# Taking the two softmax halves of block one's attention in turns

## The chip, the cores and the metric

The kernel runs on one core of a Trainium2 chip. The metric is the device time of one execution in microseconds. A core has five engines with instruction queues of their own, each worked off in the order in which the program wrote it: TensorE (PE) for matmuls, VectorE (DVE), ScalarE (ACT), GpSimd (POOL) and SyncE (SP), which issues the transfers of the weights. They wait for one another through semaphores.

## The reference

Two transformer blocks run one after the other on 256 tokens of width 1024. The change is in the first block's mixer. Its input projection feeds three things: an attention with three dilation groups and four heads, an RWKV-7 time mixing with eight heads, and the gates that merge the two.

```python
z = u @ w_in[i]                                  # attention, RWKV and gate columns
s = einsum('bqhd,bqjhd->bqhj', qb, kg) * scale   # for each of 3 groups
s = where(valid, s, -inf)
m = max(s);  e = exp(s - m);  den = sum(e);  o = e @ v / den;  lse = m + log(den)
alpha = softmax(stack(lses))                     # the three groups merged
o = alpha[0] * o0 + alpha[1] * o1 + alpha[2] * o2
...
merged = sigmoid(gate_attn) * (o_attn @ w_attn_up) + sigmoid(gate_rwkv) * (o_rwkv @ w_rwkv_up)
```

Weighting the groups with alpha is the same as one softmax over the scores of all three groups side by side, with masks. The kernel computes it that way.

## The kernel before

Attention is worked off in four rounds: query block `i` (0 or 1, 128 queries each) times head pair `hh` (0 or 1). A round holds two heads, the halves `par` 0 and 1. The scores of one half are 384 columns wide in the rounds of query block 0 and 768 in those of query block 1. The text calls the rounds (0,0), (0,1), (1,0) and (1,1).

Every engine has an `attention()` generator of the same steps, in which each `yield` ends a step:

- **Scores step.** TensorE writes the scores of both halves to PSUM (L1258). VectorE adds the mask and takes the row minimum of the negated, scaled scores for both halves (L2811; two pieces for each half in query block 1, the event is called `r`). ScalarE takes the exponential of both halves with a row sum (L1726, event `x`).
- **Next step.** VectorE waits for `x` of each half, takes the reciprocal of the row sum (L2818) and scales the half (L2417, event `e`). TensorE and ScalarE do nothing for attention here.
- **Two transpose steps**, one for each half. TensorE waits for `e` of that half and transposes it (L707), and ScalarE copies it out of PSUM (L1729, event `t`).
- **An empty step and the value step** (L1301), which ScalarE copies out.

`turns.paired(gates(), attention())` sets one step of the gate projection (six matmuls, L701 to L703) ahead of each attention step, and `turns.mix` alternates these with the steps of `rwkv()`, in the part looked at here strictly one for one. Since the generators of all engines are driven by the same sequence of turns, this sequence is also the order on each engine's queue, and an engine never passes an instruction that waits. In the RWKV chain, one step solves a level with matmuls L1131 and L1134, VectorE masks the result in two instructions (L2744, event `T`), the next step multiplies with L1147 and its neighbours, and ScalarE copies it out (event `X`). VectorE also makes the low parts of the gate weights, 1024 columns at a time (L2471, "split" below).

PSUM banks go round in rings. Attention takes them from `pa` = banks 2, 3, 4, and RWKV from `rw_bank` = banks 4, 5, 6, 7. So bank 4 is in both rings. TensorE keeps in `free[b]` the event that releases bank b and waits for it before it writes the bank again. In query block 1 the scores of a round lie in three banks, released so (`bs` are the three banks, the pairs are half and piece):

```python
for b, event in zip(bs, ((0, 0), (1, 0), (1, 1))):
    free[b] = [at_dve.at("r", i, hh, *event)]
```

In round (1,0) `bs` is 3, 4, 2, and in round (1,1) it is 2, 3, 4. The waits that this puts on TensorE ahead of the RWKV product L1147, two steps behind the scores, are `r` of half 1, piece 0 in round (1,0), and `r` of half 1, piece 1 in round (1,1), each beside `T`.

Of the kernel before, what the change touches and what calls it, by code (L numbers as in the profile page):

```python
# [242 lines left out]
def bc(ap, n):  # L243
    return ap.unsqueeze(2).broadcast_to([ap.shape[0], ap.shape[1], n])
# [30 lines left out]
def program(nc, A, consts, vecs, pt, out):  # L275
    with ExitStack() as ctx:
# [54 lines left out]
        def const(off, n):  # L331
            return low[:, OC + off:OC + off + n]
# [1383 lines left out]
        def scalar_program(e, turns):  # L1716
# [3 lines left out]
            def bank(b):  # L1720
                return PSUM[:, b, :]

            def act(o, a, f, bias=0.0, scale=1.0, accum=None):
                if accum is None:
                    return e.activation(o, a, f, bias=bias, scale=scale)  # L1725
                return e.activation(o, a, f, bias=bias, scale=scale, accum_out=accum)  # L1726

            def copy(o, a):
                return e.activation(o, a, ACT.Copy)  # L1729
# [294 lines left out]
            def attention():  # L2024
                yield
                for i in range(2):
                    for hh in range(2):
                        W, nb = 128 * (i + 1), 3 * (i + 1)
                        for _ in range(i + 2):
                            next(pa)  # L2030
                        for par in range(2):
                            q.wait_ge(*at_dve.at("r", i, hh, par, i))
                            s = at_sm[par][:, 0:3 * W]
                            act(s, s, ACT.Exp, scale=-1.0, bias=sm_at[par][0][:, i:i + 1], accum=sm_at[par][1]) \
                                .then_inc(at_act.up("x", i, hh, par), 1)
                        yield
                        yield
                        for par in range(2):
                            for b0 in range(0, nb, 4):
                                k = min(4, nb - b0)  # L2040
                                p = bank(next(pa))
                                q.wait_ge(*at_pe.at("t", i, hh, par, b0))
                                copy(at_eT[par][:, 128 * b0:128 * (b0 + k)], p[:, 0:128 * k]).then_inc(at_act.up("t", i, hh, par, b0), 1)
                            yield
                        yield
                        p = bank(next(pa))
                        q.wait_ge(*at_pe.at("o", i, hh))
                        copy(o_attn[:, hh, 128 * i:128 * i + 128], p[:, 0:128]).then_inc(at_act.up("o", i, hh), 1)
                        yield
# [16 lines left out]
            def fills():  # L2066
                yield from qkv()
                yield from turns.paired(gates(), attention())
                for _ in range(4):
                    turns.go("up", ups)  # L2070
                    yield
# [335 lines left out]
        def vector_program(e, turns):  # L2407
# [3 lines left out]
            def bank(b):  # L2411
                return PSUM[:, b, :]
# [3 lines left out]
            def ts(o, a, s1, s2, op0, op1):  # L2416
                return e.tensor_scalar(o, a, s1, s2, op0, op1) if op1 is not None else e.tensor_scalar(o, a, s1, None, op0)  # L2417
# [370 lines left out]
            def attention():  # L2788
                ma = const(C_MA, 768)
                yield  # L2790
                for i in range(2):
                    for hh in range(2):
                        W, nb = 128 * (i + 1), 3 * (i + 1)
                        bs = [bank(next(pa)) for _ in range(i + 2)]
                        for par in range(2):
                            sm = at_sm[par]
                            nm, den, rden = sm_at[par]
                            q.wait_ge(*at_pe.at("s", i, hh, par))
                            if i == 0:
                                pieces = [(bs[par][:, 0:384].rearrange("p (g t) -> p g t", g=3),  # L2800
                                           ma.rearrange("p (g w t) -> p g w t", g=3, w=2)[:, :, 1, :],
                                           sm[:, 0:384].rearrange("p (g t) -> p g t", g=3))]
                            elif par == 0:
                                pieces = [(bs[0], ma[:, 0:512], sm[:, 0:512]), (bs[1][:, 0:256], ma[:, 512:768], sm[:, 512:768])]
                            else:
                                pieces = [(bs[1][:, 256:512], ma[:, 0:256], sm[:, 0:256]), (bs[2], ma[:, 256:768], sm[:, 256:768])]
                            for n, (ps, mask, dst) in enumerate(pieces):
                                if n:
                                    q.wait_ge(*at_dve.at("r", i, hh, par, n - 1))
                                    q.wait_ge(*at_pe.at("s", i, hh, 1))  # L2810
                                e.tensor_tensor_reduce(dst, ps, mask, -0.125, 3e38 if n == 0 else nm[:, n - 1:n], ALU.add, ALU.min,  # L2811
                                                       nm[:, n:n + 1]).then_inc(at_dve.up("r", i, hh, par, n), 1)
                        yield
                        for par in range(2):
                            sm = at_sm[par]
                            nm, den, rden = sm_at[par]
                            q.wait_ge(*at_act.at("x", i, hh, par))
                            e.reciprocal(rden, den).then_inc(at_dve.up("rd", i, hh, par), 1)  # L2818
                            q.wait_ge(*at_dve.at("rd", i, hh, par))
                            ts(sm[:, 0:3 * W], sm[:, 0:3 * W], rden, None, ALU.mult, None).then_inc(at_dve.up("e", i, hh, par), 1)  # L2820
                        yield
                        for par in range(2):
                            for b0 in range(0, nb, 4):
                                next(pa)
                            yield
                        yield
                        next(pa)
                        yield
# [23 lines left out]
            def fills():  # L2852
                yield from qkv()
                yield from turns.paired(gates(), attention())
                for _ in range(4):
                    turns.go("up", ups)
                    yield
# [193 lines left out]
            def maxima(done_d, done_p, name, E, banks, W, mask, nm):  # L3051
                for h in range(4):
                    q.wait_ge(*done_p.at(name[0], h % 2))
                    o = 256 * (h // 2)
                    e.tensor_tensor_reduce(E[:, h, :], banks[h % 2][:, o:o + W], mask, -0.125, 3e38, ALU.add, ALU.min, nm[:, h:h + 1]) \
                        .then_inc(done_d.up(name[0], h), 1)

            def scaled(done_a, done_d, name, E, W, den, rden, gate):
                q.wait_ge(*done_a.at(name[1], 3))
                e.reciprocal(rden, den).then_inc(done_d.up(name[2], "r"), 1)  # L3060
                q.wait_ge(*done_d.at(name[2], "r"))
                if gate is not None:
                    tt(rden, rden, gate, ALU.mult).then_inc(done_d.up(name[2], "g"), 1)
                    q.wait_ge(*done_d.at(name[2], "g"))
                tt(E, E, bc(rden, W), ALU.mult).then_inc(done_d.up(name[2]), 1)
# [570 lines left out]
```

## Time and profile before

| | |
|---|---|
| median of 3 runs | 964.19 us (964.15 to 964.5) |
| time of the profiled execution | 963.96 us |
| its span, first to last instruction | 962.1 us |
| granted TensorE clock, mean | 0.998 |
| attention rounds of the first block | about 154 to 234 us into the span |

The span is 1.86 us shorter than the time of the same execution. The profiled execution is 0.23 us below the median. All rows below are of the profiled execution; a row's time is counted from the start of the span.

### The profile page before, as it was taken

The page shows a single profiled execution, that of the slowest core. Times are in us where ns is not written, and L with a number is a line of the kernel's source. Part 1 is how long each engine was busy: PE and PEld are TensorE (multiplying, and loading weights), DVE is VectorE, ACT ScalarE, POOL GpSimd, SP SyncE. Part 2 cuts the span into 40 slices and gives each one's busy share as a digit, 9 for nine tenths or more (in the row PEclk, how much of TensorE's full clock was granted, in tenths as well). Part 3 has the DMA queues.
Part 4 walks back from the last instruction along what each step waited for, and adds up shares of the span by engine and source line. Part 5 has one row for each costly group of instructions (what it writes and reads, how often), then busy time and mean ns, then how long its engine had stood idle before and what let it go on. Part 6 is the DMA issues. An engine that isn't in the chain of part 4 may idle for free.

```text
span 962.1 us, 15665 instructions
## 1 busy us (share of the span) xinstructions
PE 930.7 (97%) x6744; PEld 765.4 (80%) x6744; DVE 574.3 (60%) x906; ACT 427.2 (44%) x682; POOL 43.9 (5%) x60
## 2 busy tenths in 40 slices
PE   7999999999999999999999999999999999999997
PEld 5999887777658988888879988765677698888885
DVE  1568765754373566655764567865572456666673
ACT  2674344355132344444642446463341435554571
POOL 1010000100000000000000350000000000000000
PEclk9999999999999999999999999999999999999999
DMA  9445332222545855555347674433456456665531
GB/s 336 124 129 174 95 126 89 63 72 89 204 170 191 244 177 185 204 181 198 122 161 167 153 227 132 132 112 107 169 182 171 131 156 177 186 195 189 178 128 44
DMA packets 131205, 150.79 MB, mean 157 GB/s; under 512 B 11808, under 2 KB 102176, under 8 KB 131008
## 3 DMA queue, kind: packets, MB, share of 16 engines
q1 hardware_dynamic: 129920, 145.57, 48.7%
q10 hardware_dynamic: 1216, 4.23, 1.2%
q8 instruction: 53, 0.87, 0.4%
q14 instruction: 16, 0.13, 0.0%
HBM read 148.73 MB, written 1.05 MB: 156 GB/s over the span
## 4 chain that ended last, share of the span: by engine, by line
PE 83%; DVE 8%; DMA 3%; ACT 3%; issue 2%; SPq 0%; POOL 0%; POOLq 0%; ACTq 0%
PE psum L812 11%; PE psum L701 9%; PE psum L703 8%; PE psum L702 8%; PE psum L764 6%; PE psum L813 6%; PE psum L784 4%; PE psum L1315 3%; PE psum L785 3%; PE psum L793 3%; PE psum L707 2%; PE psum L870 2%; DMA low<-in_w_in_dram 2%; PE psum L860 2%; PE psum L861 2%
## 5 line engine op out<-in xcount | busy, mean ns | idle before, releaser
L1729 ACT ACTIVATE parts<-low 128x1024 fp32r<-128x1024 f32 (+1 forms) x232 | 235.5, 1047 | 107.4 <-PE psum L703 61.5
L2471 DVE TENSOR_TENSOR parts<-low,parts 128x1024 fp32r<-128x1024 f32 (+1 forms) x146 | 177.3, 1240 | 32.2 <-ACT parts L1729 31.7
L701 PE MATMUL psum<-parts 128*128 128x512 f32 (+2 forms) x424 | 171.1, 404 | 1.0 <-DVE parts L2471 1.0
L703 PE MATMUL psum<-parts 128*128 128x512 f32 (+2 forms) x424 | 163.7, 386 | 0.0
L702 PE MATMUL psum<-parts 128*128 128x512 f32 (+2 forms) x424 | 163.5, 386 | 0.0
L812 PE MATMUL psum<-parts 128*128 128x512 f32 x434 | 155.7, 398 | 0.0
L813 PE MATMUL psum<-parts 128*128 128x256 f32 x496 | 129.2, 281 | 0.0
L1729 ACT ACTIVATE high<-psum 128x512 f32<-128x512 f32 (+4 forms) x102 | 55.8, 565 | 165.0 <-PE psum L815 73.1
L813 PEld LDWEIGHTS psum<-parts 128*128 128x128 f32 x496 | 93.7, 189 | 5.7
L701 PEld LDWEIGHTS psum<-parts 128*128 128x128 f32 x424 | 79.6, 188 | 21.3 <-issue 3.2
L812 PEld LDWEIGHTS psum<-parts 128*128 128x128 f32 x434 | 81.7, 188 | 16.9
L703 PEld LDWEIGHTS psum<-parts 128*128 128x128 f32 x424 | 79.7, 188 | 16.3
L702 PEld LDWEIGHTS psum<-parts 128*128 128x128 f32 x424 | 79.8, 188 | 15.1 <-issue 1.2
L2531 DVE TENSOR_TENSOR parts<-low,parts 128x1024 fp32r<-128x1024 f32 x54 | 66.0, 1221 | 35.3 <-ACT parts L1729 35.3
L764 PE MATMUL psum<-low 128*128 128x128 f32 (+2 forms) x640 | 73.4, 276 | 2.5 <-DVE low L2448 2.4
L764 PEld LDWEIGHTS psum<-low 128*128 128x128 f32 (+2 forms) x640 | 71.9, 188 | 4.2 <-DVE low L2448 3.3
L784 PE MATMUL psum<-parts 128*128 128x256 f32 x264 | 70.0, 300 | 2.1 <-ACT parts L1729 2.1
L785 PE MATMUL psum<-parts 128*128 128x256 f32 x264 | 65.3, 283 | 0.0
L784 PEld LDWEIGHTS psum<-parts 128*128 128x128 f32 x264 | 50.3, 191 | 6.3 <-issue 5.0
L785 PEld LDWEIGHTS psum<-parts 128*128 128x128 f32 x264 | 50.5, 191 | 1.0 <-issue 1.0
L2894 DVE TENSOR_TENSOR mid<-psum,high 128x512 f32<-128x512 f32 x31 | 21.4, 691 | 44.8 <-ACT high L1729 44.8
L860 PE MATMUL psum<-parts 128*128 128x512 f32 x96 | 39.1, 407 | 2.0 <-ACT parts L1725 1.0
(313 smaller groups left out, 1293.9 us busy)
## 6 DMA issues: line engine op xcount, KB each, us to landing
low<-in_w_in_dram SPq DMA_DIRECT2D x40, 1024.0 KB, 5.2
low<-in_w_ffn_in_dram SPq DMA_DIRECT2D x44, 512.0 KB, 5.2
low<-in_w_ff_in_dram SPq DMA_DIRECT2D x16, 1024.0 KB, 5.7
low<-in_w_ff_out_dram SPq DMA_DIRECT2D x16, 1024.0 KB, 4.9
low<-in_w_ffn_out_dram SPq DMA_DIRECT2D x11, 1024.0 KB, 4.9
low<-in_w_out_dram SPq DMA_DIRECT2D x8, 1024.0 KB, 6.3
low<-in_w_ple_gate_dram SPq DMA_DIRECT2D x4, 1024.0 KB, 4.9
low<-in_w_up_dram SPq DMA_DIRECT2D x3, 1024.0 KB, 4.9
```

Source lines behind the costliest of these rows:

```text
L701: mm(o, l[0], r[0], start, False)
L702: mm(o, l[0], r[1], False, False)
L703: return mm(o, l[1], r[0], False, stop)
L764: t = mm(PSUM[0:m, banks[n], 256 * j + 128 * i:256 * j + 128 * i + 128], w3[:, k, off:off + m], uT[:, k, 128 * i:128 * i + 128], k == 0, k ...
L784: mm(o, hi[:, k, c], st.uh[:, k, :], k == 0, False)
L785: mm(o, lo_[:, k, c], st.uh[:, k, :], False, False)
L812: mm(p, hi[:, k, c], st.u2(k), k == 0, False)
L813: mm(p[:, 0:256], lo_[:, k, c], st.uh[:, k, :], False, False)
L860: mm(PSUM[:, banks[n % 2], :], l, hi[:, c], k == 0, False)
L1729: return e.activation(o, a, ACT.Copy)
L2471: tt(rslot3(n, nk, width)[:, r, 0:w], slot3(n, nk, width)[:, r, 0:w], st.hi3(j)[:, r, 0:w].bitcast(F32), ALU.subtract) \
L2531: tt(rview(OR + 2048 * n + 1024 * (k % 2), 1024), slot(n)[:, 1024 * (k % 2):1024 * (k % 2) + 1024], rview(base, 1024).bitcast(F32), ALU.su ...
```

## The change

On VectorE the masked minimum of the second half leaves the scores step and goes to the step behind it, where the scaling of the first half follows; the scaling of the second half goes one step further, to the first transpose step, behind the RWKV step in between. On ScalarE the exponential of the second half goes two steps further, again to the first transpose step, ahead of the copy. TensorE's instructions and their order stay as they are. No instruction is added or taken away.

```diff
--- before.py
+++ after.py
@@ -2028,13 +2028,17 @@
                         W, nb = 128 * (i + 1), 3 * (i + 1)
                         for _ in range(i + 2):
                             next(pa)
-                        for par in range(2):
+
+                        def weights(par):
                             q.wait_ge(*at_dve.at("r", i, hh, par, i))
                             s = at_sm[par][:, 0:3 * W]
                             act(s, s, ACT.Exp, scale=-1.0, bias=sm_at[par][0][:, i:i + 1], accum=sm_at[par][1]) \
                                 .then_inc(at_act.up("x", i, hh, par), 1)
-                        yield
-                        yield
+
+                        weights(0)
+                        yield
+                        yield
+                        weights(1)
                         for par in range(2):
                             for b0 in range(0, nb, 4):
                                 k = min(4, nb - b0)
@@ -2792,7 +2796,8 @@
                     for hh in range(2):
                         W, nb = 128 * (i + 1), 3 * (i + 1)
                         bs = [bank(next(pa)) for _ in range(i + 2)]
-                        for par in range(2):
+
+                        def maxima(par):
                             sm = at_sm[par]
                             nm, den, rden = sm_at[par]
                             q.wait_ge(*at_pe.at("s", i, hh, par))
@@ -2810,16 +2815,23 @@
                                     q.wait_ge(*at_pe.at("s", i, hh, 1))
                                 e.tensor_tensor_reduce(dst, ps, mask, -0.125, 3e38 if n == 0 else nm[:, n - 1:n], ALU.add, ALU.min,
                                                        nm[:, n:n + 1]).then_inc(at_dve.up("r", i, hh, par, n), 1)
-                        yield
-                        for par in range(2):
+
+                        def scaled(par):
                             sm = at_sm[par]
                             nm, den, rden = sm_at[par]
                             q.wait_ge(*at_act.at("x", i, hh, par))
                             e.reciprocal(rden, den).then_inc(at_dve.up("rd", i, hh, par), 1)
                             q.wait_ge(*at_dve.at("rd", i, hh, par))
                             ts(sm[:, 0:3 * W], sm[:, 0:3 * W], rden, None, ALU.mult, None).then_inc(at_dve.up("e", i, hh, par), 1)
+
+                        maxima(0)
+                        yield
+                        maxima(1)
+                        scaled(0)
                         yield
                         for par in range(2):
+                            if par == 1:
+                                scaled(1)
                             for b0 in range(0, nb, 4):
                                 next(pa)
                             yield
```

Line numbers behind the edits rise by 4 on VectorE (L2417 becomes L2421, L2471 L2475, L2744 L2748), by 5 for L2811 and L2818 (now L2816 and L2823).

VectorE in round (0,1), from the RWKV normalisation on; `ISA` is the masked minimum and the read-out of its result, RECIPROCAL and TENSOR_SCALAR on `mid` are the scaling of one half, `parts` are the low parts of gate weights. Before:

```order
L2693 TENSOR_TENSOR high<-high,low 128x512
L2818 RECIPROCAL low<-low 128x1
L2417 TENSOR_SCALAR mid<-mid,low 128x384
L2818 RECIPROCAL low<-low 128x1
L2417 TENSOR_SCALAR mid<-mid,low 128x384
L2727 TENSOR_TENSOR high<-psum,low 128x4x128 x2
L2471 TENSOR_TENSOR parts<-low,parts 128x1024
L2734 TENSOR_TENSOR high<-psum,low 128x512 x2
L2697 TENSOR_REDUCE low<-high 128x8
L2417 TENSOR_SCALAR low<-low 128x8
L2471 TENSOR_TENSOR parts<-low,parts 128x1024
```

The same place with the change:

```order
L2816 ISA mid,low<-psum,low 128x384
L2816 ISA low 128x1
L2823 RECIPROCAL low<-low 128x1
L2421 TENSOR_SCALAR mid<-mid,low 128x384
L2731 TENSOR_TENSOR high<-psum,low 128x4x128 x2
L2475 TENSOR_TENSOR parts<-low,parts 128x1024
L2738 TENSOR_TENSOR high<-psum,low 128x512 x2
L2701 TENSOR_REDUCE low<-high 128x8
L2421 TENSOR_SCALAR low<-low 128x8
L2475 TENSOR_TENSOR parts<-low,parts 128x1024
L2823 RECIPROCAL low<-low 128x1
L2421 TENSOR_SCALAR mid<-mid,low 128x384
```

The first half's scaling now stands behind the second half's minimum (the two ISA rows), and the second half's scaling has moved from the fourth and fifth row of before to behind two splits, both parts of the RWKV masking of L2731, one of L2738 and a reduction.

VectorE in round (1,0), from the first half's second minimum on. Before:

```order
L2811 ISA mid,low<-psum,low 128x256
L2811 ISA low 128x1
L2811 ISA mid,low<-psum,low 128x256
L2811 ISA low 128x1
L2811 ISA mid,low<-psum,low 128x512
L2811 ISA low 128x1
L2744 TENSOR_TENSOR high<-psum,low 64x512 x2
L2709 TENSOR_TENSOR high<-high 128x4x128
L2711 TENSOR_TENSOR high<-high 128x4x128
L2471 TENSOR_TENSOR parts<-low,parts 128x1024
L2818 RECIPROCAL low<-low 128x1
L2417 TENSOR_SCALAR mid<-mid,low 128x768
```

With the change:

```order
L2816 ISA mid,low<-psum,low 128x256
L2816 ISA low 128x1
L2748 TENSOR_TENSOR high<-psum,low 64x512 x2
L2713 TENSOR_TENSOR high<-high 128x4x128
L2715 TENSOR_TENSOR high<-high 128x4x128
L2475 TENSOR_TENSOR parts<-low,parts 128x1024
L2816 ISA mid,low<-psum,low 128x256
L2816 ISA low 128x1
L2816 ISA mid,low<-psum,low 128x512
L2816 ISA low 128x1
L2823 RECIPROCAL low<-low 128x1
L2421 TENSOR_SCALAR mid<-mid,low 128x768
```

The second half's two minima have moved behind the RWKV masking, two RWKV products and a split.

VectorE in round (1,1), before, from the RWKV masking behind the minima on:

```order
L2744 TENSOR_TENSOR high<-psum,low 64x512 x2
L2818 RECIPROCAL low<-low 128x1
L2417 TENSOR_SCALAR mid<-mid,low 128x768
L2818 RECIPROCAL low<-low 128x1
L2417 TENSOR_SCALAR mid<-mid,low 128x768
L2471 TENSOR_TENSOR parts<-low,parts 128x1024
L2744 TENSOR_TENSOR high<-psum,low 64x512 x2
L2471 TENSOR_TENSOR parts<-low,parts 128x1024
```

With the change, from the first scaling on:

```order
L2823 RECIPROCAL low<-low 128x1
L2421 TENSOR_SCALAR mid<-mid,low 128x768
L2475 TENSOR_TENSOR parts<-low,parts 128x1024
L2748 TENSOR_TENSOR high<-psum,low 64x512 x2
L2475 TENSOR_TENSOR parts<-low,parts 128x1024
L2823 RECIPROCAL low<-low 128x1
L2421 TENSOR_SCALAR mid<-mid,low 128x768
```

The second scaling has moved behind a split, the next level's masking and another split.

## Rows read from the trace of the kernel before

**Rows 1.** Page: busy time and share; granted TensorE clock in 40 slices.

```profile
PE 930.7 (97%) x6744; PEld 765.4 (80%) x6744; DVE 574.3 (60%) x906; ACT 427.2 (44%) x682; POOL 43.9 (5%) x60
...
PEclk9999999999999999999999999999999999999999
```

**Rows 2.** Windows: busy time (and count) of each engine in the rounds.

```profile
150.00:235.00 85.00, 79.33 (x1209) 61.87 (x1208) 50.37 (x94) 39.88 (x74) 2.55 (x1) 1.00 0.24 76
```

**Rows 3.** Timeline of PE: start, duration, line, forms, idle before and its releaser.

```profile
158.65 1.14 PE L1166 MATMUL psum<-high 64*64 64x64 f32 x16 [0.43 <-ACT high L1729]
...
182.72 0.55 PE L707 MATMUL psum<-low,mid 128*128 128x128 f32 x3 [0.58 <-DVE mid L2417]
...
185.76 0.49 PE L707 MATMUL psum<-low,mid 128*128 128x128 f32 x3
...
201.45 0.24 PE L1147 MATMUL psum<-high 64*64 64x64 f32 x1 [1.09 <-DVE high L2744]
...
204.67 0.88 PE L707 MATMUL psum<-low,mid 128*128 128x128 f32 x6 [0.46 <-DVE mid L2417]
...
205.47 0.27 PE L1131 MATMUL psum<-high 64*64 64x64 f32 x1
...
208.04 0.82 PE L707 MATMUL psum<-low,mid 128*128 128x128 f32 x6
...
224.15 0.24 PE L1147 MATMUL psum<-high 64*64 64x64 f32 x1 [1.10 <-DVE high L2744]
...
230.05 0.82 PE L707 MATMUL psum<-low,mid 128*128 128x128 f32 x6
```

**Rows 4.** Timeline of ACT in round (0,0).

```profile
156.67 0.62 ACT L1726 ACTIVATE mid<-mid,low 128x384 f32<-128x384 f32 x1 [4.38 <-DVE low L2811]
...
157.29 0.60 ACT L1726 ACTIVATE mid<-mid,low 128x384 f32<-128x384 f32 x1
...
158.00 1.69 ACT L1729 ACTIVATE high<-psum 64x512 f32<-64x512 f32 x3
```

**Rows 5.** Timeline of DVE in round (0,1).

```profile
177.30 0.55 DVE L2811 CUSTOM_DVE_ANT_1 mid<-psum,low 128x384 f32<-128x384 f32 x1
...
182.05 0.15 DVE L2818 RECIPROCAL low<-low 128x1 f32<-128x1 f32 x1
182.24 0.42 DVE L2417 TENSOR_SCALAR mid<-mid,low 128x384 f32<-128x384 f32 x1
...
187.54 1.22 DVE L2471 TENSOR_TENSOR parts<-low,parts 128x1024 fp32r<-128x1024 f32 x1
```

**Rows 6.** Timeline of DVE in round (1,0).

```profile
198.76 0.42 DVE L2811 CUSTOM_DVE_ANT_0 mid<-psum,low 128x256 f32<-128x256 f32 x1
...
199.22 0.75 DVE L2811 CUSTOM_DVE_ANT_0 mid<-psum,low 128x512 f32<-128x512 f32 x1
...
199.90 1.40 DVE L2744 TENSOR_TENSOR high<-psum,low 64x512 f32<-64x512 f32 x2
...
202.67 1.22 DVE L2471 TENSOR_TENSOR parts<-low,parts 128x1024 fp32r<-128x1024 f32 x1
...
203.99 0.62 DVE L2417 TENSOR_SCALAR mid<-mid,low 128x768 f32<-128x768 f32 x1
...
206.65 1.41 DVE L2744 TENSOR_TENSOR high<-psum,low 64x512 f32<-64x512 f32 x2 [1.31 <-PE psum L1134]
208.09 1.22 DVE L2471 TENSOR_TENSOR parts<-low,parts 128x1024 fp32r<-128x1024 f32 x1
```

**Rows 7.** Timeline of DVE in round (1,1).

```profile
228.66 1.41 DVE L2744 TENSOR_TENSOR high<-psum,low 64x512 f32<-64x512 f32 x2 [1.95 <-PE psum L1134]
230.10 1.23 DVE L2471 TENSOR_TENSOR parts<-low,parts 128x1024 fp32r<-128x1024 f32 x1
```

**Rows 8.** Longest waits of PE: line, waited for, us in total, times, longest.

```profile
PE psum L942 <- DMA low<-in_w_ple_dram: 5.3, 1, 5.3
...
PE psum L784 <- ACT parts L1729: 2.1, 2, 1.3
```

## The prediction

> **What bounds the kernel now.** The page comes first: TensorE is busy for 97% of the span, VectorE for 60% and ScalarE for 44% [rows 1]. So another engine counts only where TensorE waits for it, and a wait that TensorE is given in a place where it had none goes into the time whole, unless a later wait of TensorE shrinks by it. The windows narrow this to the stage of the change: in the 85 us around the four rounds TensorE is busy for 79.33 us, so at most about 5.7 us could be won in the stage at all [rows 2]. The timeline of TensorE then shows where it stands idle near the attention steps [rows 3]: 0.43 us at L1166, 0.58 us and 0.46 us at the first half's transposes of rounds (0,1) and (1,0), 1.09 us and 1.10 us at L1147 in rounds (1,0) and (1,1). It also shows what matters more: the second half's transposes L707 at 185.76, 208.04 and 230.05 us begin with no wait. The timelines of VectorE and ScalarE at the same places [rows 4 to 7] say how far ahead of these the event `e` comes, and what the change puts ahead of it.
>
> **The change part by part.** No instruction is added, and TensorE's order stays. Everything turns on four moments for each round: when `r` of the second half frees bank 4 where TensorE waits for that, and when `e` of each half comes, against the start of the transposes that wait for it. I take the rounds in order and count how much later TensorE's next work begins.
>
> *Round (0,0).* ScalarE runs two exponentials from 156.67 and 157.29 and only then, from 158.00, the copies for which L1166 waits [rows 4]. With the second exponential gone from there the copies begin about 0.6 us earlier, and TensorE's idle time of 0.43 us at L1166 [rows 3] goes. The second exponential then runs behind the copies; its transpose is some 6 us away. Term: minus 0.45 us.
>
> *Round (0,1), first half.* TensorE waits at 182.72 for `e`, which comes out of the scaling that starts at 182.24 and takes 0.42 [rows 3, 5]. VectorE is busy without a break ahead of it, and the second half's minimum, 0.55 us [rows 5], now stands right ahead of the reciprocal at 182.05. The place that it leaves at 177.30 is no gain: the RWKV masking behind it needs the matmuls of the same step, which were only just over when it began. Term: plus 0.55 us.
>
> *Round (0,1), second half.* Before, the second scaling followed right on the first. Now it stands behind the second split of the step, which starts at 187.54 and takes 1.22 [rows 5]. What is ahead of that split keeps its length: one scaling went out (0.15 and 0.42 us) and one minimum came in (0.55). So the reciprocal begins at about 188.7, the scaling 0.19 later (182.05 to 182.24), and with 0.42 `e` comes at 189.3, seen by TensorE at about 189.35. TensorE would be at its transposes at 185.76 + 0.55 = 186.3 [rows 3]. It waits for 3.05 us that it did not wait before. Term: plus 3.05 us.
>
> *Round (1,0), bank 4.* L1147 starts at 201.45 after the masking from 199.90 for 1.40 us [rows 3, 6]. The second half's two minima, from 198.76 to 199.90 with their read-outs, no longer stand ahead of that masking, so it moves up by about 1.1 us and ends at about 200.2. But L1147 also waits for the bank that the first piece of the second half's minimum frees, and this piece now stands behind the split. The split moves up by the same 1.1 us, from 202.67 to 201.6, and ends at about 202.75; the piece takes 0.42 (the row at 198.76), so L1147 starts at about 203.25, 1.8 us later than before. The 0.46 us that TensorE waited at 204.67 for the first half's `e` are gone then, since `e` comes at 202.75 + 0.46 (198.76 to 199.22) + 0.75 + 0.19 + 0.62, about 204.8, and the transposes are reached at about 206.0. Term: 1.8 minus 0.46, plus 1.35 us.
>
> *Round (1,0), second half.* Its scaling now stands behind the masking that L1131 releases. L1131 at 205.47 lets it start at 206.65, and what is behind it starts at 208.09 [rows 3, 6]. From 208.09 on, 0.19 + 0.62 bring `e` at 208.9, against transposes that were at 208.04. Both move with TensorE, so the difference stays: plus 0.9 us.
>
> *Round (1,1), bank 4 and first half.* L1147 here waits for the second piece of the second half. VectorE has the same four pieces and the same masking ahead of it in another order, with no split in between, so it ends as before and the 1.10 us at 224.15 stay, perhaps 0.1 more. The first half's `e` still comes a good 1.5 us ahead of its transposes.
>
> *Round (1,1), second half.* Its scaling now stands behind the split that starts at 230.10 and takes 1.23 [rows 7]. `e` comes at 230.10 + 1.23 - 0.1 (an instruction starts a little ahead of the end of the last) + 0.19 + 0.62, about 232.05, and with the 0.1 and the way to TensorE at 232.2, against 230.05 [rows 3]. Term: plus 2.15 us.
>
> On ScalarE the move costs nothing more: the second half's exponential stands where ScalarE would wait for the transposes, and in round (1,1), where it makes the first half's copy some 1.1 us late, the bank that this copy frees is asked for only by the transposes that are themselves 2.1 us late. Were that cover gone, about 1 us would be in the open. The splits of VectorE keep or improve their places. SyncE's transfers are released by TensorE's matmuls and move with them.
>
> **Sum.** -0.45 + 0.55 + 3.05 + 1.35 + 0.9 + 2.15 = 7.55 us. The profiled execution took 963.96 us (span 962.1 and 1.86 around it), which gives 971.5. The median of the runs is 0.23 higher than that execution, less than the terms are good for; I predict 971.5 us.
>
> **Rivals.**
>
> *Less is lost, because something gives it back (12%).* A term fails or the wait is absorbed: the piece or split ahead may have slack that the rows don't show, or a transfer that ran out just in time at a later wait. For it: two terms, 3.05 and 2.15, hang on the order behind one split each. Against it: the stage's own waits total only 5.7 us, and apart from those counted they are for copies behind the same transposes, so they move along. Without the 3.05 us the time is 968.5; without the 2.15 and the 1.35 it is 968.0.
>
> *Faster (4%).* The mechanism: if bank 4 were freed early enough, L1147 would lose its wait in rounds (1,0) and (1,1), since its masking is done 1.1 us sooner, and L1166 its 0.43: 0.45 + 1.1 + 1.1, about 2.65 us, 961.3. It decides where all of VectorE's work that now stands ahead of a second scaling ends before TensorE reaches that half's transposes. From first to second transposes TensorE takes 185.76 - 182.72 = 3.0 us and 208.04 - 204.67 = 3.4 us, and ahead of the second scaling VectorE now has, in round (0,1), two splits (2.4 us) with RWKV's own instructions between them, and in rounds (1,0) and (1,1) a masking of 1.4 us that itself begins only when TensorE has finished L1131 (206.65 against 205.47). This speaks against it, as does the piece that frees bank 4 and stands behind a split.
>
> *About the same (2%).* The losses would have to be a third of what I count and meet the 2.65 us of gains: 964.
>
> *The clock falls (10%).* TensorE's granted clock reads full in every slice of the page [rows 1]. But the longest wait inside the kernel, behind the transfer at its start of 5.3 us, is 1.3 us [rows 8], and the new one in round (0,1) would be 3.05, next to one of about 1.1. If the granted clock falls to 1.2 from 2.4 GHz there, the work behind it takes twice as long for a time. No row shows how long; with one step to one and a half (3.0 us from first to second transposes) at half speed it is 971.5 + 3 to 4.5, 974.5 to 976. The rows can't decide it, since none has such a wait in the middle; the 5.3 us ahead of the first matmul are followed by slices at full clock, which speaks for no fall.
>
> The Trainium skill, "TensorE: Matmul & The Clock Gate", section "HAM oscillation — how this bites in real kernels", says that idle gaps in the matmul stream let the gate halve the clock, and that short gaps do not. By that rule the new gap of round (0,1) is the one to ask about, and this is the rival's reason; the trace agrees in so far as none of its waits of up to 1.3 us cost any clock.
>
> **How the numbers follow.** A difference of 0.2% (1.9 us) is about what a measurement of this kernel can tell from none. The forecast of 971.5 has 72%, and its terms are good to about 0.3 us each, so 969.5 to 973.0 with all of them off one way in part. The cases: 72% forecast, 12% less lost (966.5 to 969.5), 10% clock (974.5 to 976), 4% faster, 2% the same. The range 968.0 to 974.0 takes in the forecast's own, the better part of the second case and leaves out the last two and most of the clock. Slower by over 0.2%: 94%; within: 2%; faster: 4%.
>
> **What would show it.** In the profile of the changed kernel, TensorE's waits should grow by two groups: L707 for L2421, about 1.1 and 3 us in round (0,1), 0.9 us in (1,0) and about 2.1 us in (1,1), and L1147 in round (1,0) for L2816 with about 2.9 us, no longer for L2748. L1166's wait for ScalarE should be gone, and L1147's wait in (1,1) should be about 1.1 us. From 240 us on the two timelines should be shifted by a constant. The prediction is wrong if L707 of the second half starts without a wait anywhere, if L1147 of round (1,0) starts as soon as its masking is done, or if the shift shrinks behind the stage.

## The result and the profile after

The changed kernel takes 976.08 us (median of 4 runs, 974.84 to 976.74), the kernel before 964.17 us in the same comparison. The ratio is 1.0122, with a 95% interval of 1.0105 to 1.014: 11.9 us slower. The profiled execution took 975.91 us with a span of 974.1 us, 12.0 us longer than before, and its mean granted clock is 0.993, where it was 0.998. One run of the experiments, the fourth of the rotated ring, took 1330.82 us at a mean clock of 0.654 and is left out of all that follows.

The page has TensorE's busy share at 96% in place of 97%, and 4.5 us more of busy time for the same 6744 matmuls [rows 1].

```profile
PE 935.2 (96%) x6744; PEld 768.4 (79%) x6744; DVE 574.7 (59%) x906; ACT 427.1 (44%) x682; POOL 43.9 (5%) x60
...
PEclk9999999999999999999999999999999999999999
```

The timeline of TensorE in the rounds, to be laid beside [rows 3]:

```profile
158.33 1.14 PE L1166 MATMUL psum<-high 64*64 64x64 f32 x16
...
161.96 1.14 PE L1176 MATMUL psum<-high 64*64 64x64 f32 x16 [0.58 <-ACT mid L1729]
...
183.01 0.55 PE L707 MATMUL psum<-low,mid 128*128 128x128 f32 x3 [1.18 <-DVE mid L2421]
...
188.99 0.55 PE L707 MATMUL psum<-low,mid 128*128 128x128 f32 x3 [2.79 <-DVE mid L2421]
...
190.12 2.08 PE L1107 MATMUL psum<-high 64*128 64x256 f32 x8 [0.58 <-ACT mid L1729]
...
208.07 0.27 PE L1147 MATMUL psum<-high 64*64 64x64 f32 x1 [2.94 <-DVE low L2816]
...
214.90 0.88 PE L707 MATMUL psum<-low,mid 128*128 128x128 f32 x6 [0.75 <-DVE mid L2421]
...
231.13 0.27 PE L1147 MATMUL psum<-high 64*64 64x64 f32 x1 [1.17 <-DVE low L2816]
...
239.09 0.87 PE L707 MATMUL psum<-low,mid 128*128 128x128 f32 x6 [1.88 <-DVE mid L2421]
```

L1166 waits no more (its row has no bracket). Every wait that the prediction named is there, at the line and behind the line that it named. The reader should also look at the duration of L1107: eight matmuls take 2.08 us here, and took 1.13 in the kernel before:

```profile
186.83 1.13 PE L1107 MATMUL psum<-high 64*128 64x256 f32 x8 [0.58 <-ACT mid L1729]
```

VectorE's timeline shows what stands ahead of the late events, to be laid beside [rows 5 to 7]: the split ahead of the second scaling of round (0,1), the split ahead of the piece that frees bank 4 in (1,0), and the split ahead of the second scaling of (1,1).

```profile
187.19 1.22 DVE L2475 TENSOR_TENSOR parts<-low,parts 128x1024 fp32r<-128x1024 f32 x1
188.33 0.15 DVE L2823 RECIPROCAL low<-low 128x1 f32<-128x1 f32 x1
188.52 0.42 DVE L2421 TENSOR_SCALAR mid<-mid,low 128x384 f32<-128x384 f32 x1
...
206.34 1.22 DVE L2475 TENSOR_TENSOR parts<-low,parts 128x1024 fp32r<-128x1024 f32 x1
207.59 0.42 DVE L2816 CUSTOM_DVE_ANT_0 mid<-psum,low 128x256 f32<-128x256 f32 x1
...
237.08 1.23 DVE L2475 TENSOR_TENSOR parts<-low,parts 128x1024 fp32r<-128x1024 f32 x1
```

The windows of the same execution (the third number from the end is the granted clock, 1.00 for 2.4 GHz and 0.5 for 1.2 GHz) show what the page's forty slices are too coarse for:

```profile
185.00:190.00 5.00, 1.75 (x9) 0.95 (x7) 3.87 (x8) 0.42 (x1) 2.55 (x1) 0.99 0.00 0
190.00:195.00 5.00, 4.88 (x39) 3.42 (x41) 1.29 (x2) 0.66 (x2) 0.00 (x0) 0.67 0.00 0
...
240.00:250.00 10.00, 9.57 (x117) 7.60 (x118) 1.92 (x2) 4.21 (x9) 0.00 (x0) 0.83 0.33 107
...
775.00:780.00 5.00, 4.01 (x23) 3.80 (x22) 2.83 (x6) 2.10 (x3) 0.55 (x1) 0.70 1.08 286
```

Three times the clock went down to 1.2 GHz for a while (a "fall" below): at 190 us, 0.9 us after TensorE had resumed from the wait of 2.79 us, at 241 us, 2.0 us after the wait of 1.88 us, and once at 777 us, far behind the stage. Behind the longest wait, the 2.94 us of L1147, the clock stayed full. The mean clock of a run has to be read with one thing in mind: the profiles also read 1.2 GHz in the last few us, behind TensorE's last matmul. In the kernel before this is the only such stretch, and it alone makes its mean 0.998:

```profile
957.00:962.00 5.00, 0.00 (x0) 0.00 (x0) 0.98 (x3) 1.09 (x3) 0.55 (x1) 0.68 0.29 107
```

For the fall at 777 us, the same matmuls in the kernel before and in the changed one, by their timelines. Before:

```profile
766.27 5.60 PE L764 MATMUL psum<-low 128*128 128x128 f32 x48 [0.99 <-DVE low L2448]
...
782.92 0.35 PE L784 MATMUL psum<-parts 128*128 128x256 f32 x1 [1.25 <-ACT parts L1729]
```

Changed:

```profile
776.62 7.22 PE L764 MATMUL psum<-low 128*128 128x128 f32 x48 [0.99 <-DVE low L2452]
...
794.90 0.35 PE L784 MATMUL psum<-parts 128*128 128x256 f32 x1 [1.25 <-ACT parts L1729]
```

The distance between the timelines grows there from 10.35 to 11.98 us, so this fall cost 1.6 us.

**Where the 12.0 us are.** Distances are those between equal instructions of the two traces. The stage begins with a distance of 0.18 (VectorE's minimum of round (0,0), 156.07 before and 156.25 now), which is nothing of the change.

| | distance grows | |
|---|---|---|
| round (0,0) | -0.5 | L1176 from 162.28 to 161.96 |
| round (0,1), first half | +0.6 | L707, 182.72 to 183.01 |
| round (0,1), second half | +2.9 | L707, 185.76 to 188.99 |
| first fall of the clock | +1.5 | first minimum of (1,0), 197.62 to 202.38 |
| round (1,0), both terms | +2.1 | L707, 208.04 to 214.90 |
| round (1,1), both terms | +2.2 | L707, 230.05 to 239.09 |
| second fall | +1.5 | 9.1 us at 240 us, 10.6 us at 500 us |
| third fall, and small changes after 700 us | +1.4 | 12.0 us at 783 us |

The waits make 7.3 us of it, the falls and what is beside the last of them 4.4; 0.2 was there at the start.

### The profile page after: what moved, and what is told of

The parts are those of the page before. It is cut to its first block, busy times and chain, and to the rows that moved or that the text cites. A ratio compares the mean times of both kernels' runs of the same rounds, so it can differ in the third digit from the quotient of the medians.

```text
span 974.1 us, 15665 instructions
## 1 busy us (share of the span) xinstructions
PE 935.2 (96%) x6744; PEld 768.4 (79%) x6744; DVE 574.7 (59%) x906; ACT 427.1 (44%) x682; POOL 43.9 (5%) x60
## 4 chain that ended last, share of the span: by engine, by line
PE 83%; DVE 9%; DMA 3%; ACT 2%; issue 2%; SPq 0%; POOL 0%; POOLq 0%; ACTq 0%
PE psum L812 10%; PE psum L701 9%; PE psum L702 8%; PE psum L703 8%; PE psum L764 7%; PE psum L813 6%; PE psum L784 4%; PE psum L1315 3%; PE psum L785 3%; PE psum L793 3%; PE psum L707 2%; PE psum L870 2%; DMA low<-in_w_in_dram 2%; PE psum L860 2%; PE psum L861 2%
## 5 line engine op out<-in xcount | busy, mean ns | idle before, releaser
L2475 DVE TENSOR_TENSOR parts<-low,parts 128x1024 fp32r<-128x1024 f32 (+1 forms) x146 | 177.3, 1240 | 32.2 <-ACT parts L1729 31.8
```

The source lines that it names most:

```text
L2475: tt(rslot3(n, nk, width)[:, r, 0:w], slot3(n, nk, width)[:, r, 0:w], st.hi3(j)[:, r, 0:w].bitcast(F32), ALU.subtract) \
```

## The experiments

Two theories were open about the size. One: the waits are what VectorE's order makes them, and the falls of the clock follow from the waits. The other: one of the named terms is not what it seems (bank 4, or the late scaling), or the clock falls on its own. All times are compared with the kernel before run on the same chip, 963.98 to 964.07 us. "Profile" is the one profiled execution of each kernel. The diffs are against the changed kernel and show only the lines that matter; where scalings or minima move on VectorE, the second exponential moves with them on ScalarE.

The mean clocks of the other runs say only roughly how often the clock fell, and not where. The kernel before has such runs too: in the three comparisons 8 of its 49 runs read 0.997 and took 965.2 to 966.2 us, where the others took 963.4 to 964.5 us, although its profile has no wait longer than 1.3 us behind TensorE's first matmul.

**One half of the change: the minima in turns.** The second exponential goes one step behind the scores, and both scalings stay together there.

```diff
                         maxima(1)
                         scaled(0)
+                        scaled(1)
                         yield
                         for par in range(2):
-                            if par == 1:
-                                scaled(1)
```

> Half of the change: the minima take turns (second half's minimum and exponential one step behind the scores), but both scalings stay together in that step. Theory (the loss is VectorE's order: three late scalings and one late release of bank 4, and the clock falls because of the waits): round (0,0) -0.4, round (0,1) first half +0.6, round (1,0) release of bank 4 +1.4 net with L1147 waiting about 2.9 us, no wait at any second-half transposes; sum +1.6, so 965.8 us, plus about 1.7 us for each fall of the clock, of which at most one is expected. Rival (the clock falls come with any shift of the program and not with the waits): the same sum and three falls, 970.5 us or more.

Measured: 966.83 us (965.02 to 967.32, 10 runs), ratio 1.0024 (1.0015 to 1.0034). The profile is of the shortest run, with a span 1.1 us longer than before and a clock of 0.998; most other runs read 0.996 or 0.997 and 966.7 to 967.3 us. No second-half transposes wait, and L1147 in (1,0) does:

```profile
203.43 0.27 PE L1147 MATMUL psum<-high 64*64 64x64 f32 x1 [2.95 <-DVE low L2816]
```

The sum of 1.6 us was right to 0.5 us in the profile, which has no fall. That the 8 longer of the 10 runs had one is read from their mean clocks alone, and where it was is not shown; at 8 of 10 such runs are far more frequent than the 8 of 49 of the kernel before. So the same kernel costs 1.1 us in one run and 2.7 to 3.3 us in another.

**The other half: the second scaling late.** Minima and exponentials stay in the scores step.

```diff
                         maxima(0)
+                        maxima(1)
                         yield
-                        maxima(1)
                         scaled(0)
```

> The other half: both minima and both exponentials stay in the scores step, but the second half's scaling moves to the first transpose step. Theory: second-half transposes wait about 2.8 us in round (0,1), 0.8 us in (1,0) and 1.9 us in (1,1), L1147 in (1,0) waits 1.1 us as before; sum +5.5, so 969.7 us without the clock, and 1.7 us more for each fall: one right behind the 2.8 us wait, 971.4 us, up to 973. Rival (the late second minimum is what hurts): under 966 us.

Measured: 975.76 us (972.79 to 977.16, 4 runs), ratio 1.0113 (1.0092 to 1.0135), with clocks of 0.990 to 0.995. The profile, again of the shortest run, has a span of 971.0 us and two falls:

```profile
188.78 0.55 PE L707 MATMUL psum<-low,mid 128*128 128x128 f32 x3 [2.93 <-DVE mid L2421]
...
213.65 0.87 PE L707 MATMUL psum<-low,mid 128*128 128x128 f32 x6 [0.76 <-DVE mid L2421]
...
237.77 1.47 PE L707 MATMUL psum<-low,mid 128*128 128x128 f32 x6 [1.89 <-DVE mid L2421]
```

```profile
190.00:195.00 5.00, 5.00 (x42) 3.49 (x44) 1.29 (x2) 0.68 (x1) 0.00 (x0) 0.66 0.00 0
...
235.00:240.00 5.00, 2.85 (x25) 1.95 (x25) 2.62 (x5) 0.87 (x2) 0.00 (x0) 0.79 0.00 0
240.00:245.00 5.00, 5.00 (x68) 4.16 (x65) 0.81 (x2) 3.10 (x5) 0.00 (x0) 0.87 0.15 24
```

By the distances between equal matmuls the waits make 6.1 us of this profile's longer span and the two falls 2.9 (1.65 and 1.25), against 5.5 expected for the waits. That the median is 975.8 and not 971 to 973 was a miss: I had allowed for one fall. The profiled run has two, and the longest run, 4.4 us above it at a clock of 0.990, has room for almost three more; that it had them is read from its mean clock alone. The rival that the late minimum hurts alone is out: this half is the larger.

**One late scaling alone.** The kernel before, with only round (0,1)'s second scaling late. The line shown is the one that keeps it late; the other lines go back to the kernel before.

```diff
-                        if par == 1:
+                        if par == 1 and (i, hh) == (0, 1):
```

> The kernel before with a single edit: in round (0,1) the second half's scaling moves to the first transpose step. It makes one wait of about 2.9 us in place of none. Theory: 2.9 us of wait, so 967.0 us, and 1.7 us more in the runs in which the clock falls behind it, 968.7. Rival (the late scaling is covered): 964 us.

Measured: 969.76 us (968.75 to 970.68, 4 runs), ratio 1.0056 (1.0043 to 1.007). The profile:

```profile
188.92 0.55 PE L707 MATMUL psum<-low,mid 128*128 128x128 f32 x3 [2.93 <-DVE mid L2424]
...
190.04 1.82 PE L1107 MATMUL psum<-high 64*128 64x256 f32 x8 [0.58 <-ACT mid L1729]
```

The wait is 2.9 us and the span 4.8 us longer: one instruction of 0.42 us and its reciprocal, put behind two splits and the RWKV work between them, cost 2.9 us directly and 1.9 us more in this profile, with a fall at 190 us. By the medians they cost 5.7 us, 1 us more than the 968.7 expected with one fall. The other runs, 0.9 to 1.9 us longer, read clocks of 0.994 and 0.995.

**The changed kernel without that one.**

```diff
                         scaled(0)
+                        if (i, hh) == (0, 1):
+                            scaled(1)
```

> The changed kernel, with the second half's scaling of round (0,1) alone back beside the first (and its exponential one step behind the scores). Theory: the 2.8 us wait at the second transposes of (0,1) is gone, 4.1 us stay, so 968.0 us without a fall; each fall adds 1.7 us; with the wait ahead of 190 us gone the fall there is gone too, and those behind the 2.9 us wait of (1,0) or the 1.9 us wait of (1,1) may come: 968 to 971.5. Rival (that scaling is not the largest term): over 973 us.

Measured: 969.91 us (969.42 to 972.83, 4 runs), ratio 1.0068 (1.0053 to 1.0084), 6.2 us under the changed kernel. The fall at 190 us is gone, and there is one at 204 us, 0.9 us after L1147's wait of 2.96 us; none follows the wait of 1.89 us in (1,1):

```profile
200.00:205.00 5.00, 2.04 (x67) 1.49 (x67) 4.70 (x10) 0.74 (x2) 0.00 (x0) 0.93 0.01 3
205.00:210.00 5.00, 5.00 (x47) 3.98 (x47) 0.55 (x1) 3.58 (x8) 0.00 (x0) 0.73 0.25 56
```

**Another owner for bank 4.** The changed kernel with the attention's ring started at bank 3, on all engines.

```diff
-            pa, pg = itertools.cycle((2, 3, 4)), itertools.cycle((0, 1))
+            pa, pg = itertools.cycle((3, 4, 2)), itertools.cycle((0, 1))
```

> The changed kernel with the attention's ring of PSUM banks started at bank 3 (3, 4, 2 instead of 2, 3, 4), so that bank 4 holds the first half's second piece in round (1,0) and the second half's first piece in (1,1). Theory: L1147 in (1,0) no longer waits for L2816 (2.9 us gone), but the first transposes there then wait about 1.7 us for their scaling; net -1.2 us; in (1,1) L1147's wait shrinks from 1.2 to about 0.5 us; the waits of 0.4 to 0.6 us for copies out of bank 4 change places; together 2 to 4 us less than the changed kernel, 972 to 974 us. Rival (bank 4 is not what L1147 waits for there): the 2.9 us wait stays and the time is 976.

Measured: ratio 1.0063 (1.0046 to 1.008) from three runs, at 969.66, 969.93 and 971.9 us. The 2.94 us wait of L1147 in (1,0) is gone, and the first transposes behind it wait in its place, by the amount expected; L1147 in (1,1) waits 0.39 us:

```profile
183.81 0.52 PE L707 MATMUL psum<-low,mid 128*128 128x128 f32 x3 [2.48 <-DVE high L2731]
...
189.63 0.55 PE L707 MATMUL psum<-low,mid 128*128 128x128 f32 x3 [1.08 <-DVE mid L2421]
...
208.11 0.88 PE L707 MATMUL psum<-low,mid 128*128 128x128 f32 x6 [1.74 <-DVE mid L2421]
...
228.25 0.27 PE L1147 MATMUL psum<-high 64*64 64x64 f32 x1 [0.39 <-DVE low L2816]
```

So bank 4 is what L1147 waited for. What I had not worked out is the first row: in round (0,1) the first transposes now go to bank 4 and wait until VectorE has emptied it of an RWKV product. The gain came out larger than expected all the same, since only one fall is left in this profile, at 185 us.

**Filling one wait.** The changed kernel with eleven useless matmuls ahead of the long wait in round (0,1); the transposes overwrite them.

```diff
+                                if (i, hh, par) == (0, 1, 1):
+                                    for _ in range(11):
+                                        mm(p, st1.uh[:, 0, 0:128], ..., True, True)
+                                    q.wait_ge(*at_dve.at("e", i, hh, par))
```

> The changed kernel, with eleven 128x512 matmuls of no use (2.5 us, overwritten by the transposes) on TensorE in round (0,1) ahead of the wait for the second half's scaling, where it stood idle for 2.8 us. Nothing else changes. Theory (the clock fell because TensorE stood idle): the granted clock stays full from 190 to 195 us, L1107 takes 1.13 instead of 2.08 us, and the time falls by about 1.7 us to 974.3, more if later falls go too. Rival (the clock falls on its own): the clock in that stretch is at 1.2 GHz again and the time is 976.

Measured: 973.62 us (972.83 to 974.84, 4 runs), 2.5 us under the changed kernel, ratio to before 1.0096 (1.0081 to 1.0112). L1107 takes 1.13 us and the clock stays at 1.00 from 185 to 195 us. But now it falls in the next long wait, 1.3 us before its end:

```profile
206.57 0.37 PE L1147 MATMUL psum<-high 64*64 64x64 f32 x1 [2.95 <-DVE low L2821]
```

```profile
205.00:206.00 1.00, 0.00 (x0) 0.00 (x0) 1.00 (x1) 0.00 (x0) 0.00 (x0) 0.86 0.00 0
...
205.00:210.00 5.00, 3.43 (x68) 3.02 (x69) 2.94 (x7) 1.39 (x3) 0.00 (x0) 0.57 0.00 2
210.00:215.00 5.00, 5.00 (x48) 3.96 (x46) 1.17 (x2) 2.91 (x6) 0.00 (x0) 0.74 0.48 139
```

This stretch at 1.2 GHz lasts until 212.6 us and costs 2.7 us by the distance between L1147 and the second L707 of the round (9.55 us, where the changed kernel has 6.83 without a fall). At 244 us the profile is therefore only 0.3 us ahead of the changed kernel; 1.6 of its 1.9 us come from there being no fall at 777 us. That the filled wait has no fall behind it is shown; that filling it alone is worth 2.5 us is not, since this hangs on where the clock falls otherwise.

**Filling all of them.** The same in all six longer waits of the rounds (4, 11, 11, 2, 4 and 7 matmuls; those ahead of L1147 go to the other bank of its pair).

> The changed kernel, with matmuls of no use (128x512, overwritten afterwards) in each of TensorE's six longer waits of the rounds: 4 and 11 ahead of the transposes of round (0,1), 11 ahead of L1147 and 2 ahead of the second transposes in (1,0), 4 and 7 in (1,1), each a little shorter than the wait. The waits' length stays what VectorE's order makes it. Theory (the falls of the clock come from TensorE standing idle): no fall from 180 to 245 us in any run, and the time is the changed kernel's without its falls, 969.0 + 1.9 = 971 us, with little spread. Rival (the falls have nothing to do with the waits): 974 to 977 us as before.

Measured: 971.77 us (970.86 to 973.02, 4 runs), ratio 1.0078 (1.0065 to 1.0092), 4.3 us under the changed kernel with 39 matmuls more. Work that nobody needs made the kernel faster. The mean clock is 0.998 in three of four runs, 0.997 in one. The distance of L707 of round (1,1) to before is 237.70 - 230.05 = 7.65 us, where the changed kernel has 9.04 with a fall in it:

```profile
189.01 0.55 PE L707 MATMUL psum<-low,mid 128*128 128x128 f32 x3 [0.31 <-DVE mid L2429]
...
237.70 0.88 PE L707 MATMUL psum<-low,mid 128*128 128x128 f32 x6 [0.27 <-DVE mid L2429]
```

The events from VectorE come no earlier than in the changed kernel; only TensorE's idling is taken away, and the falls go with it, the one at 777 us too in this profile. The time left is the sum of the waits.

All profiles together, outside the last few us: TensorE has 13 unfilled waits of 1.88 to 2.96 us in the rounds, and the clock fell at 8 of them (at one in the wait, at the others up to 2.0 us after it). At the other five (2.95 us in the half with the minima in turns, 2.94 in the changed kernel, 1.89 to 1.91 in the rotated ring, the single filled wait and the changed kernel without that one scaling) it stayed full. The only other fall is that at 777 us. The five profiles without such a wait (before, all waits filled, the first round alone twice, and the version for speed below) have none. So a fall needs no more than such a wait, but does not always follow it, and nothing in the profiles speaks for the rival that a mere shift of the program brings the falls.

**The first round alone, twice.** The change in round (0,0) only.

> The change in round (0,0) alone; the other three rounds as before. Theory: TensorE's 0.43 us wait at L1166 is gone and nothing else changes: 0.3 to 0.5 us faster than before, 963.7 us, no fall of the clock. Rival (the start of the rounds carries a cost of its own): 964.0 us or more.

> The change in round (0,0) alone, measured again beside the version above: 963.5 us, 0.4 to 0.6 us under before, if the first measurement was no chance; 964.0 us if it was.

Measured: 963.49 us against 964.07, ratio 0.9994 (0.9985 to 1.0003), and again 963.53 against 963.98, ratio 1.0 (0.9991 to 1.0009). TensorE's wait at L1166 is gone from the profile. The half microsecond shows in both medians and in neither interval.

**A version for speed.** What the runs say is worth having: round (0,0) changed, (0,1) and (1,0) as before, and in (1,1) the minima in turns with both scalings one step behind the scores, and with bank 4 given to the piece that is read first.

```diff
                         bs = [next(pa) for _ in range(i + 2)]
+                        if (i, hh) == (1, 1):
+                            bs = [bs[2], bs[0], bs[1]]
```

> A version for speed: the change whole in round (0,0); rounds (0,1) and (1,0) as before; in round (1,1) the minima take turns but both scalings stay one step behind the scores, and the three score banks are dealt 4, 2, 3 instead of 2, 3, 4, so that bank 4 is freed by the first half's first minimum. Theory (order on VectorE and the owner of bank 4 decide): L1166's wait of 0.43 us and L1147's of 1.10 us in (1,1) both go: 0.4 + 1.0, so 962.6 us, ratio 0.9985. Rival (L1147 there was not held by its masking's place, or the transposes behind take the wait over): 963.6 us, as with the first round alone.

Measured: 962.42 us (961.99 to 963.96, 11 runs) against 963.98, ratio 0.9981 (0.9972 to 0.999). It is 1.6 us under the kernel before, where 1.4 were expected, and 13.7 under the changed one. L1147 in (1,1) has no wait, and the masking L2755 for it stands between the minima; the scaling behind them waits 0.36 us for the second exponential, which costs TensorE nothing:

```profile
220.85 1.41 DVE L2755 TENSOR_TENSOR high<-psum,low 64x512 f32<-64x512 f32 x2
222.29 0.42 DVE L2825 CUSTOM_DVE_ANT_0 mid<-psum,low 128x256 f32<-128x256 f32 x1
...
224.61 0.17 DVE L2832 RECIPROCAL low<-low 128x1 f32<-128x1 f32 x1 [0.36 <-ACT mid L1728]
```

## Why the prediction was wrong

Slower was right, and so was the sum of the waits; the time came out above the range because of the clock.

- *Round (0,0), -0.45:* right, -0.5.
- *Round (0,1), +0.55 and +3.05:* right, +0.6 and +2.9. The one late scaling alone makes a wait of 2.9 us.
- *Round (1,0), +1.35 and +0.9:* right, +2.1 together. Bank 4 is the cause of the first, by the rotated ring, with L1147's wait at 2.94 us where I said about 2.9.
- *Round (1,1), a rest of 0.1 and +2.15 with it:* right, +2.2.
- *Nothing for ScalarE, splits and transfers:* right; the second exponential is never waited for. "From 240 us on shifted by a constant" was wrong, by the clock at 241 and 777 us.
- *"The clock falls (10%)"* is the step that failed, in chance and in size. I took it for a single fall, only behind the 3 us wait, with one in ten. The sum has no term for it. The runs show 12 of 12 executions of the three kernels with the late scaling of round (0,1) unfilled (the changed one, the half with all late scalings, the one late scaling) at mean clocks of 0.990 to 0.997, where 41 of 49 runs of the kernel before read 0.998 or 0.999, and falls behind waits of 1.9 us as well. The changed kernel has three falls in its profile, of 1.5, 1.5 and 1.6 us, which with small changes beside the last make 4.4 of the 12.0 us, and its four runs read clocks of 0.993 to 0.996, the shortest the highest. The rival's price for a single fall, 3 to 4.5 us, was too high: it took the work behind for a whole step at half speed. Its 974.5 to 976 are near the measured time because three falls at half that price add up to about the same, which is luck. The forecast without the clock, 971.5, is what the kernel with all waits filled measures, 971.77. Had I taken falls behind each of the waits of 1.9 to 3 us as likely, the sum would have been 971.5 + 3 x 1.6 = 976.3. That this meets the measured time is luck too: in the profile only two of the three waits have a fall, and the third fall is the one at 777 us.
- The reason given against it, that 5.3 us ahead of the first matmul were followed by a full clock, carried nothing: a slice of 24 us reads 9 with a fall in it as well, as the changed kernel's page shows. The windows of the kernel before do read 1.00 from 0 to 20 us, but TensorE had done nothing ahead of that stretch, so it is no wait in the middle of work.

The page "TensorE: Matmul & The Clock Gate" of the Trainium skill, section "HAM oscillation — how this bites in real kernels", ties the falls to gaps in the matmul stream; the filled waits show just that here. Its rule looks at the length of a single gap, and by it all waits of the rounds, the longest 2.96 us, would be harmless: the traces do not agree, with falls at 190 us behind 2.79 and 2.93 us and at 238 and 241 us behind 1.9 us.

Open stays why the clock fell at 777 us in one profile, behind waits of 0.8 and 1.0 us that the kernel before has too without a fall, which of several waits is followed by a fall in a given run (the same kernel, minima in turns, took 965.0 us in one run and 967.3 in another), and what lowers the mean clock in 8 of 49 runs of the kernel before, none of which was profiled.

## What to carry to other kernels

Work moved from a stretch where an engine's order is tight to "the step behind" lands behind everything that this step puts first. Before moving it, look up on the consumer's timeline when it asks for the result, and on the producer's what now stands ahead. A ring of banks shared by two streams makes the order in which one stream's tiles are read a matter of the other's progress; dealing the shared bank to the tile that is read first, together with the minima in turns in round (1,1), gained 1.1 us here (962.42 against 963.53 us) with no instruction moved on TensorE; what either gains alone was not measured. And a new wait of about 2 us or more in a stream of matmuls can cost more than its length: here one of 2.9 us cost 5.7 us by the medians, and waits of 7.3 us together cost 11.9.

## What was not expected of the hardware

Adding 39 matmuls of no use took 4.3 us off the changed kernel. The clock falls at waits of 1.9 to 3.0 us of TensorE, at 8 of 13 of them and at different places from kernel to kernel (185, 190, 204, 205, 238 and 241 us), and once, at 777 us, behind none. A fall costs 1.3 to 1.7 us by the distances between equal matmuls, and in one profile 2.7 us.
